# Gate and up of two feed-forward parts: the high weights times high and low inputs in one product of 512 columns, the halves added by ScalarE and VectorE

## The reference, cut to what matters

```python
def swiglu(h, w_gate, w_up, w_down):
    return (jax.nn.silu(h @ w_gate) * (h @ w_up)) @ w_down
...
def _conv_glu(h, w_up, conv_w, conv_b, w_down):
    u = _causal_dwconv(h @ w_up, conv_w) + conv_b
    gate, up = jnp.split(u, 2, axis=-1)
    return (jax.nn.silu(gate) * up) @ w_down
```

## Time and profile before

| | us |
|---|---|
| median of 3 runs | 1834.43 |
| lowest and highest of them | 1834.2 and 1839.47 |
| the profiled execution, its own time | 1839.33 |
| its span, first to last instruction | 1837.6 |
| TensorE busy | 1794.9 |
| VectorE busy | 1405.8 |
| ScalarE busy | 1131.7 |

### The profile page before, as it was taken

How to read it: one execution, slowest core, us unless ns; L and a number is a source line. 1 busy time by engine, 2 the same in 40 slices (tenths; PEclk the granted TensorE clock), 3 DMA queues, 4 the chain that set the end, 5 groups by cost and what they waited for, 6 DMA issues and landing times.

```text
span 1837.6 us, 25765 instructions
## 1 busy us (share of the span) xinstructions
PE 1794.9 (98%) x9992; PEld 1551.8 (84%) x9992; DVE 1405.8 (76%) x1164; ACT 1131.7 (62%) x942; POOL 116.7 (6%) x133
## 2 busy tenths in 40 slices
PE   8999999999999999999999999999999898899999
PEld 6789999898888888888888888888888797689998
DVE  6475445655988989898889888898898867677775
ACT  6444444463776777777777777767677544645553
POOL 7000000000000000000000000000000028210000
PEclk9999999999999999999999999999999999789999
DMA  7446565432998998998989989989999543225561
GB/s 234 161 139 196 172 206 183 161 138 81 356 386 310 388 367 323 385 369 324 375 329 375 368 321 385 368 327 381 343 355 370 199 141 135 69 86 189 184 200 54
DMA packets 244356, 479.27 MB, mean 261 GB/s; under 512 B 11759, under 2 KB 80137, under 8 KB 244249
## 3 DMA queue, kind: packets, MB, share of 16 engines
q1 hardware_dynamic: 243385, 476.43, 72.3%
q10 hardware_dynamic: 864, 1.31, 0.2%
HBM read 476.66 MB, written 1.05 MB: 260 GB/s over the span
## 4 chain that ended last, share of the span: by engine, by line
PE 89%; DVE 5%; POOL 2%; ACT 2%; issue 1%; DMA 0%; DVEq 0%; ACTq 0%; SPq 0%; POOLq 0%
PE bank L1978 28%; PE bank L1980 27%; PE bank L1979 27%; PE bank L2297 1%; PE bank L2329 1%; POOL arena L820 1%; DVE wl L438 1%; DVE xT L1295 1%; DVE xTl L1238 1%; POOL arena L821 1%; PE bank L2366 0%; PE bank L1947 0%; PE bank L2367 0%; DVE h L1308 0%; DVE xn L1251 0%
## 5 line engine op out<-in xcount | busy, mean ns | idle before, releaser
L1978 PE MATMUL bank<-wh,xTh 128*128 128x512 f32 x1568 | 622.2, 397 | 11.1 <-DVE arena L1334 5.4
L1980 PE MATMUL bank<-wh,xTl 128*128 128x512 f32 x1568 | 613.1, 391 | 0.0
L1979 PE MATMUL bank<-wl,xTh 128*128 128x512 f32 x1568 | 612.5, 391 | 0.0
L1542 DVE TENSOR_TENSOR wl<-raw,wh 128x2048 fp32r<-128x2048 f32 x224 | 512.1, 2290 | 92.6 <-ACT wh L1024 91.0
L1024 ACT ACTIVATE wh<-raw 128x2048 fp32r<-128x2048 f32 x224 | 429.2, 1918 | 120.7 <-PE bank L1980 120.7
L1978 PEld LDWEIGHTS bank<-wh,xTh 128*128 128x128 f32 x1568 | 295.8, 189 | 74.2 <-DVE arena L1334 5.6
L1980 PEld LDWEIGHTS bank<-wh,xTl 128*128 128x128 f32 x1568 | 295.6, 189 | 62.9
L1979 PEld LDWEIGHTS bank<-wl,xTh 128*128 128x128 f32 x1568 | 296.1, 189 | 58.6
L438 DVE TENSOR_TENSOR wl<-raw,wh 128x2048 fp32r<-128x2048 f32 x112 | 255.4, 2298 | 68.3 <-ACT wh L431 66.5
L1978 PE MATMUL bank<-xTh,wh 128*128 128x256 f32 x1024 | 292.1, 285 | 1.2 <-DVE xTl L1238 0.8
L1980 PE MATMUL bank<-xTh,wl 128*128 128x256 f32 x1024 | 290.9, 284 | 0.0
(11 more groups left out here) (379 smaller groups left out, 1397.3 us busy)
## 6 DMA issues: line engine op xcount, KB each, us to landing
raw<-in_moe_w_up SPq DMA_DIRECT2D x112, 1024.0 KB, 7.6
arena<-in_moe_w_gate SPq DMA_DIRECT2D x96, 1024.0 KB, 7.5
raw<-in_moe_w_down SPq DMA_DIRECT2D x96, 1024.0 KB, 7.1
raw<-in_w_up SPq DMA_DIRECT2D x22, 1024.0 KB, 5.8
raw<-in_moe_w_gate SPq DMA_DIRECT2D x16, 1024.0 KB, 7.4
arena<-in_moe_w_down SPq DMA_DIRECT2D x16, 1024.0 KB, 7.2
raw<-in_gla_w_in SPq DMA_DIRECT2D x12, 1024.0 KB, 8.0
raw<-in_w_in SPq DMA_DIRECT2D x12, 1024.0 KB, 6.2
```

The lines of the kernel that those rows point to most:

```text
L1542: V.tensor_tensor(wl[:, s, :], moe_raw(c)[0], wh[:, s, :].bitcast(F32), ALU.subtract).then_inc(lo_moe, 1)
L1978: T.matmul(o, xh, yh, start=first, stop=False)
L1979: T.matmul(o, xh, yl, start=False, stop=False)
L1980: return T.matmul(o, xl, yh, start=False, stop=last)
```

## The change

High and low halves of the normed input, `xTh` and `xTl`, become the two halves of one tensor `xhl`. In gate and up of both parts a k now has two products: the high weights times the high and low inputs side by side (512 columns), and the low weights times the high inputs (256 columns), which go on top of the left half. A bank then holds one block of 128 hidden columns, its left half the sum of two products and its right half the third. Gate takes banks 0 and 1, up banks 2 and 3, in every step. ScalarE copies the right half of each bank to SBUF (`right_half`), and VectorE adds the left half to it (`both_halves`, tensor `f_gu`), which lets the bank go. The taps of `f2` then read `f_gu` and not the bank.

```diff
+        xhl = sb("xhl", [P, 2, KD, S], F32R)
+        xTh, xTl = xhl[:, 0], xhl[:, 1]
...
             def gu(j):
-                turn((f, j, "g"), 2 * (j % 2))
-                turn((f, j, "u"), 2 * (j % 2) + 1)
+                for i, kind in enumerate("gu"):
+                    for b in range(2):
+                        turn((f, j, kind, b), 2 * i + b)
...
+                    def right_half(i):
+
+                        for b in range(2):
+                            at_ = slice((2 * i + b) * S, (2 * i + b + 1) * S)
+                            A(V.activation(f_gu[:, j % 2, at_], see(act, (f, j, "gu"[i], b))[:, S:2 * S], ACT.Copy), "right")
+
+                    if j >= 2:
+                        act.wait_ge(sg("act_" + f), j - 1)
+                    right_half(0)
                     if conv:
...
+                                gone(act, (f, j, "gu"[i], b))
+                                A(V.activation(f_cu[:, j % 2, at_], f_gu[:, j % 2, at_], ACT.Identity,
+                                               scale=col("tap2", k), bias=col("conv_b", k)), "conv0")
+
+                        last_tap(0)
                         hi.upto(min(pos[f, j, "g"] + NW, len(pieces) - 1))
-                        gone(act, (f, j, "g"))
-                        A(V.activation(f_sg[:, j % 2, :], f_cu[:, j % 2, 0:512], ACT.Silu), "silu_" + f)
-                        last_tap(1, see(act, (f, j, "u")))
+                        act.wait_ge(sg("taps_" + f), 4 * j + 2)
+                        A(V.activation(f_sg[:, j % 2, :], f_cu[:, j % 2, 0:512], ACT.Silu), "silu")
+                        right_half(1)
+                        last_tap(1)
                     else:
...
+                        for b in range(2):
+                            gone(act, (f, j, "g", b))
+                        A(V.activation(f_sg[:, j % 2, :], f_gu[:, j % 2, 0:512], ACT.Silu), "silu")
+                        right_half(1)
...
+                def both_halves(j, i):
+
+                    for b in range(2):
+                        lab = (f, j, "gu"[i], b)
+                        at_ = slice((2 * i + b) * S, (2 * i + b + 1) * S)
+                        dve.wait_ge(sg("right"), 4 * (base(f) + j) + 2 * i + b + 1)
+                        C(V.tensor_tensor(f_gu[:, j % 2, at_], see(dve, lab)[:, 0:S], f_gu[:, j % 2, at_], ALU.add), frees=lab)
+
...
-                            ps = see(dve, (f, j, "gu"[i]))
-                            dve.wait_ge(sg("conv0"), 4 * j + 2 * (i + 1))
+                            both_halves(j, i)
+                            if i == 0:
+                                lo.upto(min(pos[f, j, "g"] + NW, len(pieces) - 1))
...
-                            if i == 0:
-                                lo.upto(min(pos[f, j, "g"] + NW, len(pieces) - 1))
...
+                            for part in (0, 1) if k < KD - 1 else (1, 0):
+                                if part == 0:
+                                    ins = T.matmul(ps[:, :].rearrange("p (a s) -> p a s", a=2), h_[:, k, bs], xhl[:, :, k, :],
+                                                   start=(k == 0), stop=(k == KD - 1))
+                                else:
+                                    T.matmul(ps[:, 0:S], l_[:, k, bs], xTh[:, k, :], start=False, stop=False)
```

More of the change, by code:

```diff
@@ L1477, in ffn @@
-                            if i == 0:
-                                lo.upto(min(pos[f, j, "g"] + NW, len(pieces) - 1))
-                        dve.wait_ge(sg("silu_" + f), j + 1)
-                        lhs, rhs = f_sg[:, j % 2, :], f_cu[:, j % 2, 512:1024]
-                    else:
-                        gone(dve, (f, j, "g"))
-                        lhs, rhs = f_sg[:, j % 2, :], see(dve, (f, j, "u"))[:, :]
+                                C(V.scalar_tensor_tensor(cu[:, 2:S], x[:, 0:S - 2], col("tap01", k), cu[:, 2:S],
+                                                         ALU.mult, ALU.add), "taps_" + f)
@@ L1488, in ffn @@
-                    if not conv:
-                        tick(frees=(f, j, "u"))
+                    C(V.tensor_tensor(f_act[:, j % 2, :], f_sg[:, j % 2, :], rhs, ALU.mult), "act_" + f)
                     lo.upto(min(pos[f, j, "g"] + NW, len(pieces) - 1))
-                    dve.wait_ge(sg("acth_" + f), j + 1)
+                    dve.wait_ge(sg("acth"), base(f) + j + 1)
                     C(V.tensor_tensor(actl[:, j % 2, :], f_act[:, j % 2, :], acth[:, j % 2, :].bitcast(F32), ALU.subtract),
-                      "actl_" + f)
+                      "actl")
@@ L2172, in _ @@
             norm("n1", {(1, 0): 16})
-            keep(("f1", 0, "g"), 7)
+            keep(("f1", 0, "g", 0), 7)
             x_low("n1", (0, 2))
@@ L2177, in down @@
                 def down(j):
-                    pe.wait_ge(sg("actl_" + f), j + 1)
+                    pe.wait_ge(sg("actl"), base(f) + j + 1)
                     i = pos[f, j, "d"]
@@ L2194, in down, with gate_up @@
                         ins.then_inc(sg("down_done_" + f), 1)
+                def gate_up(j, kind, fresh=None):
+                    i = pos[f, j, kind]
+                    split_done(pe, i)
+                    h_, l_ = of(wh, i, KD), of(wl, i, KD)
+                    for b in range(2):
+                        ps = take((f, j, kind, b))
+                        bs = slice(b * P, (b + 1) * P)
+                        for k in range(KD):
+                            if fresh and b == 0 and k == KD // 2:
+                                x_low(fresh, (1, 3))
+                            for part in (0, 1) if k < KD - 1 else (1, 0):
[4 more added lines that the diff above has]
+                                    T.matmul(ps[:, 0:S], l_[:, k, bs], xTh[:, k, :], start=False, stop=False)
+                        done(ins, (f, j, kind, b))
                 for j in range(NJ1):
-                    fm((f, j, "g"), None if j else x)
-                    fm((f, j, "u"))
+                    gate_up(j, "g", None if j else x)
+                    gate_up(j, "u")
                     if j:
@@ L2575, in _ @@
             norm("n5", {(1, 0): 15})
-            keep(("f2", 0, "g"), 7)
+            keep(("f2", 0, "g", 0), 7)
             x_low("n5", (0, 2))
```

41 lines of the change are left out of this document (16 added, 25 removed).

## The result

The changed kernel takes 1881.96 us in the median of 4 runs (1879.87 to 1884.24), the kernel before 1834.95 us beside it. The ratio is 1.0251, 95% interval 1.023 to 1.0273: slower by 47 us, where 34.5 were forecast. 1882 us lies above the forecast's range of 1860 to 1878. The profiled execution took 1879.87 us, 2.1 under its median.

What follows compares the result with a forecast made beforehand. TensorE bounds the kernel before; after, a VectorE-ScalarE chain bounds the convolution part. 36.4 + 2.8 - 4.7 = 34.5 us more, on a median of 1834.43, gives 1869 us, range 1860 to 1878 (0.76).

Steps and rivals of the forecast that it cites:

- The chain: Second part: VectorE and ScalarE waiting on each other make a step 20.41 us against TensorE's 16.53; 36.4 us later.
- The last down: End of second part: after 6.6 us of idling, 14 products run at the 1.2 GHz level, adding 2.8 us.
- TensorE in the second part: TensorE idles about 3.1 us a step ahead of down, is busy about 81%, and adds nothing to the step.
- rival 3: TensorE's clock falls in each step's 3.1 us idling; 19.3 us a step, deciding only from 7.8 us; chance 0.03.
- a granted clock under 1 in the part's middle: Convolution (second) part: one of the signs listed as showing the forecast wrong.
- 4.7 us less: First part: TensorE stays the bound, gate and up go from 11.52 to 11.09 us in each of 11 steps.
- The last step: End of first part: next stage's weight halves go ahead of acth and actl; tight, counted 0 (bounds 0 and 1).
- VectorE and ScalarE, what is added: Each step gets four copies of 0.38 us, four additions of 0.42, and ScalarE taps from SBUF at 0.60.
- Sum: Whole kernel: 36.4 + 2.8 - 4.7 = 34.5 us more.
- Rival 2: Both parts: VectorE and ScalarE keep up, each part gains 4.7 us, 9.4 in all, 1825 us; chance 0.05.
- Rival 4: Gate and up: wide products gain nothing or a fifth, only the first part's 4.7 lost; 1873 to 1874; chance 0.05.
- Rival 1: Second part: the chain is the bound but shorter than counted; 1847 us at 18 us a step; chance 0.10.

Runs made afterwards that it cites:

- The two reordering runs: Changed kernel with VectorE's low half of the next up behind the gate's taps: 1848.1 us; changed kernel with ScalarE's second-part order mended: 1840.1 us.
- the run in another order: Change in the first part alone, products ordered wide, narrow, narrow, wide, against the kernel before: 1840.87 us beside 1837.16.
- the padded kernels: Met waits added ahead of ScalarE's expert loop: kernel before with 88 more instructions, 1845.58 us, with 44, 1835.69; changed kernel with 165 more, 1872.41.

## Why the prediction was right, and where it was not

**The chain, right.** Forecast 20.41 us a step and 36.4 in the second part; measured 20.39, and 36.5 (last `acth` ends at 1864.94, 37.8 us later than before, of which 1.3 is the later start of the part). The new prices were right as well: addition 423 ns (0.42), copy 379 (0.38), ScalarE's tap from SBUF 601 (0.60), VectorE's taps 0.48. The two reordering runs show the mechanism: one move in VectorE's queue brings the step to 17.2 us, the moves in ScalarE's bring it to TensorE's 16.72.

**The last down, right.** 2.7 us longer from the end of `actl` to the last addition to `h` (forecast 2.8): 13 products at the low level, not 14, and 4.68 us of idling ahead of them, not 6.6.

**TensorE in the second part, mechanism wrong without effect.** Forecast 3.1 us of idling ahead of down and 81% busy; measured 1.8 and 91%. The difference is what rival 3 had: the clock falls in each step. It costs 1.6 us of TensorE's time, far under the 7.8 from which it would decide. The prediction names a granted clock under 1 in the part's middle as a sign of being wrong; it came (0.93), and the chain held all the same. Rival 3 placed the loss between idling of 2.41 us, which kept the clock, and 5.42, and no such bound holds. The same gap at the start loses the clock in the changed kernel:

```profile
47.50 0.50 PE L1995 MATMUL bank<-wh,xhl 128*128 128x512 f32 x1 [2.41 <-DVE wl L442]
...
49.56 0.63 PE L1996 MATMUL bank<-wl,xhl 128*128 128x512 f32 x1
```

Window over it:

```profile
49.00:53.00 4.00, 4.00 (x12) 3.10 (x12) 3.97 (x3) 0.60 (x1) 0.00 (x0) 0.59 0.82 260
```

And in the changed kernel with 165 instructions of padding one step idles as long as here and keeps it, by its timeline:

```profile
1728.36 0.47 PE L1998 MATMUL bank<-wh,acth 128*128 128x512 f32 x1 [1.78 <-DVE wl L442]
```

Its window:

```profile
1728.00:1736.00 8.00, 7.64 (x36) 6.42 (x37) 5.04 (x5) 3.42 (x4) 0.00 (x0) 1.00 0.81 262
```

**The first part, size wrong.** The mis-sized term is "4.7 us less": the mechanism holds (no idling, additions covered), but the part is 2.6 us shorter (134.07 to 320.68 before, 133.95 to 317.98 now, first product to last). The pair takes 0.3522 and not 0.3467 us: the sum took a product's price from rows in which all products have one width, and the run in another order gives 0.13 of the missing 0.18 us of a step back. The last step and the rest cost nothing that I could see.

**The expert loop, missed.** This is the step that failed: "VectorE and ScalarE, what is added" prices what the added instructions do and not that they are there, and "Sum" has terms for the two parts alone, so the stages between them stand at nothing. 88 instructions (44 copies and 44 waits) ahead of ScalarE's loop moved its branch from 623 to 711 and cost 7.7 us. That this is the cause is shown by the padded kernels, in both directions.

**The account of the miss.** Forecast 1868.9, measured 1882.0: 13.1 us. 7.7 are the loop, 2.1 the first part. The other 3.3 lie in how the profiled executions stand to their medians. The forecast took 4.9 us off for the profiled execution of before, its slowest, and that trace has the reason, a stretch in the router stage at half clock, seen in its window:

```profile
1475.00:1480.00 5.00, 5.00 (x25) 5.00 (x25) 0.86 (x5) 1.15 (x1) 1.16 (x1) 0.50 0.36 113
```

The changed kernel has 1.00 there, and so has the kernel before with 44 instructions more, whose span is 1834.0 us against 1837.6. So the stretch makes 3.6 of the 4.9 us (one execution of each kernel), and 1.3 were taken off too much (0.5 of them is the fourth run of before, with which its median is 1834.95). The changed kernel's median then lies 2.1 above its profiled execution, and no trace shows where. Between the two profiled executions nothing is left over: 34.5 us were forecast and 40.5 measured, and 7.7 + 2.1 - 3.6 = 6.2 us is the difference of 6.0 but for rounding.

**The rivals.** Rival 2's 1825 us needed an order the change doesn't have; with ScalarE's order mended and the loop moved it is neared: 6.9 us of gain (1837.07 to 1830.14) of its 9.4. Gate and up of 11.14 for 11.09 us make 1.1 of what is missing, in 22 steps; the other 1.4 have no place, and are less than the 5.6 us over which the nine runs of before beside it spread. Rival 4 was wrong: the wide product gains 0.25 of the 0.43 us a step that the rows said. Rival 1 is out, with 20.39.

## What to carry to other kernels

Write a chain down station by station from the order of each queue whenever a bank's or buffer's reader changes; here it was right to 0.1%, and the same work in another order can be worth 34 us. Where a kernel has a real loop, instructions added ahead of it on the same engine can cost some us at its branch (7.7 here): compare stages that the diff doesn't touch, look for idling with no releaser, and read the instruction queue's packets there. Take the price of a product from rows with the same mixture of widths.

## What the hardware showed that was not expected

- A loop of 265 instructions on ScalarE, run three times, stalled for 5.7 to 6.1 us at both of its returns in all eight kernels whose branch stood at instruction 711, and in none of the six with it at 623, 667 or 876. Each stall has 4 packets of 8 KB on q14. That queue has a packet near every 128th instruction of ScalarE, one of them near 714; that the branch beside it is the reason, for a loop that begins at 447, fits all runs and isn't tested.
- The length of a gap alone doesn't say whether the clock falls. It fell after 1.82 us of idling in the second part, for 8 products, and stayed after 1.78 us at the same place in another kernel; after 2.41 us at the start it stayed in the kernel before and fell to 0.59 in the changed one. What decides it, these runs don't show.
- A wide product costs the same whether its operand is one run of 512 columns or two of 256 (11.27 us of gate and up each), but the order of wide and narrow products counts: 24 changes of width fewer in a step save 0.13 us.
